# A fused transformer kernel's last up projection: VectorE's sums of weights ahead of its other work, taps counted by chunk, and the last tile's channels read at the end

## The chip, the cores and the metric

One core of one Trainium2 chip runs the whole program. The metric is the device time of one execution in microseconds. The engines are TensorE (PE, with its weight loads as PEld), VectorE (DVE), ScalarE (ACT), GpSimd (POOL) and SyncE (SP), which issues most DMAs. Each runs its own list of instructions in order, and semaphores tie the lists together.

## What is computed

Two blocks of a small model follow each other on 256 tokens of width 1024, all in float32: a mixer (mLSTM) and a mixture of experts, a second mixer (GLA) and a second mixture of experts, then attention and a gated feed-forward network with a convolution. The change lies in the last one:

```python
def conv_ffn(y, w_up, conv_w, conv_b, w_down):
    """Gated MLP with causal depthwise conv between up-projection and activation."""
    u = y @ w_up                                   # [256,1024] @ [1024,5632]
    c = u.shape[-1]
    u = lax.conv_general_dilated(u, conv_w[:, None, :], window_strides=(1,),
                                 padding=[(CONV_WIDTH_2 - 1, 0)],
                                 dimension_numbers=('NWC', 'WIO', 'NWC'),
                                 feature_group_count=c) + conv_b
    gate, val = jnp.split(u, 2, axis=-1)
    return (jax.nn.silu(gate) * val) @ w_down      # [256,2816] @ [2816,1024]
```

CONV_WIDTH_2 is 3. The result is added to the stream, and a last RMS norm follows.

## The kernel before

**Tiles of the up projection.** The 2816 gate channels and the 2816 value channels are cut into UPT = 11 tiles of 256 of each. A tile has four chunks c of 128 channels: 0 and 1 are gates, 2 and 3 values. Tile 0 is projected alone (L1330) into banks 0 and 1. The other ten go in five pairs, `UPS`, called blocks 0 to 4 here (g in the code), each one use of a seven-product scheme: the matrices are halved along tokens, along the inner dimension and along columns, and seven products of sums and differences of the parts stand in for eight plain ones.

**TensorE.** `block_product(u, x)` (L891) issues product x in four steps k of four matmuls; the trace has two records for each matmul. The order is 1, 2, 3, 6, 5, 7, 4. Products 1 to 3 read weights as they landed. Products 6, 5, 7 and 4 read sums of weights and wait for them step by step (`weights_summed[2]`, `[1]`, `[3]`, `[4]`). Product 6 adds to the bank of product 1 and waits for the first take; product 7 adds to the same bank and waits for the fourth (`out_taken`, 9u+4). Odd and even blocks use different banks.

**Who makes the sums.** GpSimd makes the four first sums (L685) and the eight last ones (L694) of each block, one after another. VectorE makes the four second ones in `second_weight_sums` (L1728), each in place in the weights that product 3 reads, so that sum k waits for step k of product 3. GpSimd's last sums read VectorE's.

**VectorE.** `take_value(u, number, x, tt, j)` (L1768 for a copy, L1770 for an addition) brings product x out of its bank into `pre[0]` or `pre[1]`, nine takes in all for a block: takes 1 and 2 are of products 1 and 2, take 3 of 3, take 4 of 6, takes 5 and 6 of 5, takes 7 and 8 of 7 (`middle_values` is takes 4 to 8), take 9 of 4 (`last_values`). Take 1 overwrites `pre[0]`, so it waits for the convolution of the tile before that lay there. After take 7 the odd tile s = 2g+1 is whole in `pre[1]`, after take 9 the even tile s = 2g+2 in `pre[0]`.

**The convolution.** For tile s of `CONV_ORDER` = 0, 2, 1, 4, 3, 6, 5, 8, 7, 10, 9, ACT makes the middle tap and the bias of the four chunks (L1626), VectorE adds the two other taps in two passes of four steps (`convolve`, L2181), ACT takes silu of the gates (L1630), and VectorE multiplies gates and values (`gated`, L2190) into `ffh`, with one count of `ff_ready` for each tile. `conv` has two buffers, so the taps of tile s wait for `ff_ready` of s-2.

**The down projection.** `product` (L1359) is again seven products, of 11 matmuls of 512 columns each. Matmul p of product 1 reads the first of tile p's two channel blocks, and `down_step` counts six weight tiles of two matmuls each (the last has one). Product 1 waits for `ff_ready` once a weight tile, for `min(2 * i + 3, UPT)`. Product 3 waits for sums of the left operand that VectorE makes once all tiles are gated (L2213 to L2218); then VectorE makes the sums of the right operand (L2221, L2263, L2269, L2274), adds products to the stream (L2238), and the norm ends the program.

Of the kernel before, what the change touches and what calls it, by code (L numbers as in the profile page):

```python
# [18 lines left out]
ACT = mybir.ActivationFunctionType  # L19
# [121 lines left out]
def build_in(nc, t, out, ctx):  # L141
# [660 lines left out]
    def _(pe):  # L802
# [515 lines left out]
        def ffn():  # L1318
            turn_only(acc, U_FFN, 0)
            arrived(pe, T_UP)  # L1320
            w = slot(T_UP).rearrange("p (k n) -> p k n", k=KC)
            for tt in range(TT):
                for c in range(4):
                    at = (c % 2) * S + tt * P
                    if (tt, c) == (0, 3):
                        turn_only(acc, U_FFN, 1)
                    for k in range(KC):
                        if c == 0 and k % 4 == 0:
                            turned_bank(U_FFN, 2 * tt + k // 4)
                        last = mm(PS[c // 2][:, at:at + P], w[:, k, c * P:(c + 1) * P], xT[:, k, tt * P:(tt + 1) * P],  # L1330
                                  start=(k == 0), stop=(k == KC - 1), skip_group_check=True)
            last.then_inc(tile_used, 1)
            pe.wait_ge(small_landed[4], 64)
            for j in range(4):
                last = turn(PS[6][:, j * 2 * FB:(j + 1) * 2 * FB], conv_rows[:, j, :], ident[0:2 * FB, 0:2 * FB])
            last.then_inc(convT_done, 1)
            for u in UPS:
                for x in (1, 2, 3, 6, 5, 7, 4):
                    if (u, x) == (UPS[0], 3):
                        pe.wait_ge(convT_copied, 1)  # L1340
                    elif (u, x) == (UPS[1], 1):
                        pe.wait_ge(conv_done, 1)
                    block_product(u, x)

            def product(x, left, odd, half, bank, first=True):

                made = {3: 4, 4: 2, 5: 1, 6: 2, 7: 3}
                for i in range(N_DOWN):
                    if x == 1:
                        pe.wait_ge(ff_ready, min(2 * i + 3, UPT))  # L1350
                        arrived(pe, T_DOWN + i)
                    elif x == 4:
                        pe.wait_ge(right_ready[4], i + 1)
                    elif x in (5, 6, 7):
                        pe.wait_ge(right_ready[made[x]], i + 1)
                    w = right_block(i, odd, half)
                    for r in range(w.shape[1]):
                        p = 2 * i + r
                        last = mm(PS[bank][:, :], left[:, p], w[:, r], start=(first and p == 0), stop=(p == PAIRS - 1),  # L1359
                                  skip_group_check=True)  # L1360
                    last.then_inc(down_step, 1)

            pe.wait_ge(out_taken, 9 * UPS[-1] + 6)
            product(1, left_block(0, 0), 0, 0, 6)
            product(2, left_block(0, 1), 1, 0, 7)
            pe.wait_ge(left_ready, 3)
            pe.wait_ge(out_taken, 9 * (UPS[-1] + 1))
            product(3, left_sum(4), 1, 1, 4)

            pe.wait_ge(sums_taken, 1)  # L1370
            product(6, left_sum(2), 1, 1, 6, first=False)
            product(5, left_sum(1), 0, 1, 5)
            pe.wait_ge(left_ready, 4)
            pe.wait_ge(sums_taken, 4)
            product(7, left_sum(3), 0, 0, 6, first=False)
            product(4, left_block(1, 1), 1, 0, 7)
# [14 lines left out]
    def _(act):  # L1391
# [215 lines left out]
        def ffn():  # L1607
            for tt in range(TT):
                rms_root(1, tt)
                copy_turned(U_FFN, tt)  # L1610
            act.wait_ge(convT_done, 1)
            f(convw_t, PS[6][:, 0:8 * FB], ACT.Copy).then_inc(convT_copied, 1)
            act.wait_ge(convT_copied, 1)

            for s, i in enumerate(CONV_ORDER):
                if s == 0:
                    act.wait_ge(tile_used, T_UP + 1)
                else:

                    act.wait_ge(out_taken, 9 * UPS[(s - 1) // 2] + (7 if s % 2 else 9))  # L1620
                if s >= 2:
                    act.wait_ge(ff_ready, s - 1)
                for c in range(4):
                    n = 2 * i + c % 2 + FB * (c // 2)
                    src = PS[c // 2][:, (c % 2) * S:(c % 2 + 1) * S] if s == 0 else pre[s % 2][:, c]
                    last = f(conv[:, s % 2, c], src, ACT.Identity, scale=conv_cols[:, 2, n:n + 1],  # L1626
                             bias=conv_cols[:, 3, n:n + 1])
                last.then_inc(taps_done, 1)
                act.wait_ge(conv_done, s + 1)
                f(conv[:, s % 2, 0:2], conv[:, s % 2, 0:2], ACT.Silu).then_inc(ff_silu, 1)  # L1630

            f(small[:, 250:251], ones[:, 0:1], ACT.Sqrt, bias=rms_eps)
            for i, (tt, j) in enumerate(((0, 0), (0, 1), (1, 1), (1, 0))):
                c = slice(512 * j, 512 * (j + 1))
                act.wait_ge(final_sum, i + 1)
                f(acc[:, tt, c], x_tok[:, tt, c], ACT.Square, accum_out=half_squares[:, 2 * tt + j:2 * tt + j + 1]
                  ).then_inc(final_square, 1)
                if i == 1:
                    final_deviation(0)
            final_deviation(1)  # L1640
# [18 lines left out]
    def _(dve):  # L1659
# [509 lines left out]
        def ffn():  # L2169
            copy_transposes(U_FFN)  # L2170
            dve.wait_ge(convT_copied, 1)

            def convolve(s):
                i = CONV_ORDER[s]
                dve.wait_ge(taps_done, s + 1)
                for back in (1, 2):
                    for c in range(4):
                        n = 2 * i + c % 2 + FB * (c // 2)
                        u = PS[c // 2][:, (c % 2) * S:(c % 2 + 1) * S - back] if s == 0 else pre[s % 2][:, c, 0:S - back]
                        dst = conv[:, s % 2, c, back:S]  # L2180
                        last = v.scalar_tensor_tensor(dst, u, conv_cols[:, 2 - back, n:n + 1], dst, ALU.mult, ALU.add)  # L2181
                    if back == 1:
                        link(last)
                last.then_inc(conv_done, 1)

            def gated(s):
# [10 lines left out]
            for g, u in enumerate(UPS):  # L2197
                dve.wait_ge(conv_done, 2 * g + 1)
                take_value(u, 1, 1, 0, 0, None)
                gated(2 * g)  # L2200
                take_value(u, 2, 2, 0, 0)
                second_weight_sums(u)
                take_value(u, 3, 3, 0, 1, None)
                middle_values(u)
                convolve(2 * g + 1)
                last_values(u)
                gated(2 * g + 1)
                convolve(2 * g + 2)
            gated(UPT - 1)

            dve.wait_ge(ff_ready, UPT)
            dve.wait_ge(tile_used, T_UP + UPT)
# [115 lines left out]
```

## Time and profile before

| | |
|---|---|
| median of 3 runs | 1548.99 us (1548.19 to 1549.23) |
| the profiled execution | 1550.7 us, its span 1548.7 us |
| mean granted TensorE clock | 0.933 |
| busy share of the span | PE 82%, PEld 47%, DVE 33%, ACT 14%, POOL 20% |
| chain that ended last | PE 49%, DMA 38%, DVE 7% |
| up projection in five blocks, the first at | 1335.56 us |
| down projection, first matmul at | 1472.68 us |

Shares are of the whole program, whose long middle is the two mixtures of experts; what a change in the feed-forward network is worth has to be read between 1335 us and the end. All durations come from the one profiled execution. A row of the timeline may merge several instructions (xN), and its own duration then runs from the start of the first to the end of the last. Matmuls overlap each other, so a product's length is read from start to start.

### The profile page before, as it was taken

The page shows a single profiled execution, that of the slowest core. Times are in us where ns is not written, and L with a number is a line of the kernel's source. Part 1 is how long each engine was busy: PE and PEld are TensorE (multiplying, and loading weights), DVE is VectorE, ACT ScalarE, POOL GpSimd, SP SyncE. Part 2 cuts the span into 40 slices and gives each one's busy share as a digit, 9 for nine tenths or more (in the row PEclk, how much of TensorE's full clock was granted, in tenths as well). Part 3 has the DMA queues.
Part 4 walks back from the last instruction along what each step waited for, and adds up shares of the span by engine and source line. Part 5 has one row for each costly group of instructions (what it writes and reads, how often), then busy time and mean ns, then how long its engine had stood idle before and what let it go on. Part 6 is the DMA issues. An engine that isn't in the chain of part 4 may idle for free.

```text
span 1548.7 us, 21551 instructions
## 1 busy us (share of the span) xinstructions
PE 1273.6 (82%) x9321; PEld 733.3 (47%) x9321; DVE 505.3 (33%) x980; ACT 214.9 (14%) x440; POOL 313.9 (20%) x274
## 2 busy tenths in 40 slices
PE   9998977567667679999887667767768999998998
PEld 7554533223223234865533223223224784998943
DVE  2457210001001006677311000001005456567684
ACT  1032100000000001261200000000002014121110
POOL 2404000000000006574000000000001757355600
PEclk9999999889788899999998988888889999999999
DMA  9928899999999999736799999999999980444000
GB/s 347 384 96 320 331 427 427 429 427 427 428 426 427 427 419 369 304 116 231 312 427 427 428 426 427 427 427 427 427 427 388 313 264 30 160 141 186 28 0 28
DMA packets 88286, 498.89 MB, mean 322 GB/s; under 512 B 8452, under 2 KB 31392, under 8 KB 63872
## 3 DMA queue, kind: packets, MB, share of 16 engines
q1 hardware_dynamic: 85728, 490.23, 78.1%
q0 software_dynamic: 2464, 7.29, 1.5%
q8 instruction: 74, 1.21, 0.3%
q14 instruction: 20, 0.16, 0.0%
HBM read 496.42 MB, written 1.07 MB: 321 GB/s over the span
## 4 chain that ended last, share of the span: by engine, by line
PE 49%; DMA 38%; DVE 7%; another core or an unknown queue 2%; issue 1%; ACT 1%; SPq 0%; DVEq 0%; POOL 0%
DMA weight_ring<-in_moe_w_down 29%; PE bank L891 12%; PE bank L894 7%; PE bank L1182 5%; PE bank L1359 4%; PE bank L1247 4%; PE bank L1234 4%; PE bank L857 3%; DMA weight_ring<-in_moe_w_up 3%; DMA phase_room<-in_moe_w_gate 3%; DMA weight_ring<-in_moe_w_gate 3%; DVE weight_ring L1728 2%; PE bank L1157 1%; PE bank L1330 1%
## 5 line engine op out<-in xcount | busy, mean ns | idle before, releaser
L1182 PE MATMUL bank<-weight_ring,x_tok 128*32 128x256 f32 x3328 | 225.7, 420 | 111.9 <-DMA weight_ring<-in_moe_w_up 95.2
L1182 PEld LDWEIGHTS bank<-weight_ring,x_tok 128*32 128x32 f32 x3328 | 110.8, 118 | 222.4 <-issue 87.0
L1234 PE MATMUL bank<-weight_ring,xT 128*32 128x512 f32 x864 | 136.9, 765 | 75.2 <-DMA weight_ring<-in_moe_w_down 69.1
L694 POOL TENSOR_TENSOR weight_ring<-weight_ring 128x512 f32<-128x512 f32 x112 | 152.6, 1394 | 153.2 <-DVE weight_ring L1728 87.1
L685 POOL TENSOR_TENSOR weight_ring<-weight_ring 128x512 f32<-128x512 f32 x56 | 73.0, 1335 | 455.6 <-DMA weight_ring<-in_w_qkv 442.2
L2073 DVE TENSOR_TENSOR xT<-xT,bank 128x256 f32<-128x256 f32 x32 | 13.5, 421 | 460.7 <-PE bank L1182 460.7
L1247 PE MATMUL bank<-x_tok,xT 128*128 128x512 f32 x256 | 124.5, 630 | 0.0
L2078 DVE COPY x_tok<-bank 128x512 f32<-128x512 f32 x32 | 22.1, 692 | 249.9 <-PE bank L1234 249.9
L1234 PEld LDWEIGHTS bank<-weight_ring,xT 128*32 128x32 f32 x864 | 27.1, 124 | 155.4 <-DMA weight_ring<-in_moe_w_down 71.9
L1247 PEld LDWEIGHTS bank<-x_tok,xT 128*128 128x128 f32 x256 | 49.1, 203 | 87.2 <-issue 87.2
L720 POOL DMA_DIRECT2D phase_room<-in_gla_w_in x1 | 1.0, 967 | 434.2 <-PE bank L1234 434.2
L891 PE MATMUL bank<-xT,weight_ring 128*128 128x128 f32 x768 | 87.7, 275 | 0.0
L891 PEld LDWEIGHTS bank<-xT,weight_ring 128*128 128x128 f32 x768 | 86.8, 192 | 1.0 <-issue 1.0
L891 PE MATMUL bank<-acc,weight_ring 128*128 128x128 f32 x640 | 75.3, 277 | 8.9 <-DVE weight_ring L1728 8.9
L891 PEld LDWEIGHTS bank<-acc,weight_ring 128*128 128x128 f32 x640 | 72.8, 192 | 11.1 <-DVE phase_room L1770 6.8
L1182 PE MATMUL bank<-phase_room,x_tok 128*32 128x256 f32 x768 | 51.2, 416 | 23.7 <-DMA phase_room<-in_moe_w_up 17.1
L894 PE MATMUL bank<-weight_ring,xT 128*128 128x512 f32 x144 | 66.7, 609 | 2.2 <-issue 1.4
L1728 DVE TENSOR_TENSOR weight_ring<-weight_ring 128x512 f32<-128x512 f32 x56 | 65.5, 1219 | 2.4 <-PE bank L891 1.6
L857 PE MATMUL bank<-weight_ring,xT 128*128 128x512 f32 x128 | 59.0, 594 | 0.6 <-PE bank L857 0.6
L894 PE MATMUL bank<-weight_ring,acc 128*128 128x512 f32 x128 | 57.1, 597 | 1.1 <-DVE weight_ring L1728 1.1
L1554 ACT ACTIVATE xT<-bank 128x256 f32<-128x256 f32 x32 | 12.3, 384 | 272.3 <-PE bank L1209 272.3
L1182 PEld LDWEIGHTS bank<-phase_room,x_tok 128*32 128x32 f32 x768 | 25.8, 117 | 48.9 <-issue 17.7
(299 smaller groups left out, 1514.7 us busy)
## 6 DMA issues: line engine op xcount, KB each, us to landing
weight_ring<-in_moe_w_gate SPq DMA_DIRECT2D x52, 2048.0 KB, 49.7
weight_ring<-in_moe_w_up SPq DMA_DIRECT2D x52, 2048.0 KB, 49.7
weight_ring<-in_moe_w_down SPq DMA_DIRECT2D x52, 2048.0 KB, 49.3
phase_room<-in_moe_w_gate SPq DMA_DIRECT2D x12, 2048.0 KB, 48.1
phase_room<-in_moe_w_up SPq DMA_DIRECT2D x12, 2048.0 KB, 50.0
weight_ring<-in_w_up SPq DMA_DIRECT2D x22, 1024.0 KB, 10.5
phase_room<-in_moe_w_down SPq DMA_DIRECT2D x8, 2048.0 KB, 50.4
weight_ring<-in_gla_w_in SPq DMA_DIRECT2D x6, 2048.0 KB, 23.4
```

Of the source, the lines that this page charges most:

```text
L685: nc.gpsimd.tensor_tensor(a, a, b, ALU.subtract).then_inc(weights_summed[1], 1)
L694: nc.gpsimd.tensor_tensor(b, a, b, ALU.subtract).then_inc(weights_summed[x], 1)
L857: last = mm(bank[:, :], xT[:, k, tt * P:(tt + 1) * P], w[:, k, :], start=(k == 0), stop=(k == KC - 1), skip_group_check=True)
L891: last = mm(bank[:, c * P:(c + 1) * P], w[:, k, c * P:(c + 1) * P], left[:, k], start=(first and c == 0), stop=(k == HALF - 1), skip_group ...
L894: last = mm(bank[:, :], left[:, k], w[:, k], start=first, stop=(k == HALF - 1), skip_group_check=True)
L1157: last = mm(PS[quarter % 2][:, at:at + P], x_perm[:, tt, k, :], sels[g][:, tt], start=(tt == 0), stop=(tt == TT - 1))
L1182: last = mm(bank[q * CAP:(q + 1) * CAP, 0:S], xinT[:, 4 * r + k, j * CAP:(j + 1) * CAP], w[k][:, q * S:(q + 1) * S], start=(r == 0 and k = ...
L1234: last = mm(PS[i][k * CAP:(k + 1) * CAP, :], hidT[:, 4 * r + k, :], w[k][:, i * 512:(i + 1) * 512], start=(r == 0), stop=(r == 1), skip_gr ...
L1247: last = mm(PS[4 + 2 * tt + i][:, :], selT[:, tt * P:(tt + 1) * P], exp_t[:, i * 512:(i + 1) * 512], start=False, stop=True, skip_group_ch ...
L1359: last = mm(PS[bank][:, :], left[:, p], w[:, r], start=(first and p == 0), stop=(p == PAIRS - 1), skip_group_check=True)
L1728: v.tensor_tensor(a, a, b, ALU.subtract).then_inc(weights_summed[2], 1)
L2078: v.tensor_copy(exp_t[:, 512:1024], PS[1][:, :]).then_inc(exp_dve, 1)
```

## The change

Three edits of order. In the loop over blocks VectorE does the second sums of weights straight after take 1, then take 2, and then the gated products, of which the odd tile's has moved into the next block (and behind everything for the last tile). ACT counts every tap chunk, VectorE waits chunk by chunk (for tile 0 for all four), and take 9 stands between the two passes of the odd tile's convolution; ACT makes silu of an odd tile only behind the taps of the even one after it. In product 1 of the down projection each matmul waits for its own tile only, and pair 9, whose tile is convolved last, is read last.

```diff
             def product(x, left, odd, half, bank, first=True):
                 made = {3: 4, 4: 2, 5: 1, 6: 2, 7: 3}
-                for i in range(N_DOWN):
+                blocks = [(i, r) for i in range(N_DOWN) for r in range(right_block(i, odd, half).shape[1])]
+                if x == 1:
+                    blocks.append(blocks.pop(UPT - 2))
+                for i, r in blocks:
+                    p, w = 2 * i + r, right_block(i, odd, half)
                     if x == 1:
-                        pe.wait_ge(ff_ready, min(2 * i + 3, UPT))
+                        pe.wait_ge(ff_ready, CONV_ORDER.index(p) + 1)
                         arrived(pe, T_DOWN + i)
-                    elif x == 4:
+                    elif x == 4 and r == 0:
                         pe.wait_ge(right_ready[4], i + 1)
-                    elif x in (5, 6, 7):
+                    elif x in (5, 6, 7) and r == 0:
                         pe.wait_ge(right_ready[made[x]], i + 1)
-                    w = right_block(i, odd, half)
-                    for r in range(w.shape[1]):
-                        p = 2 * i + r
-                        last = mm(PS[bank][:, :], left[:, p], w[:, r], start=(first and p == 0), stop=(p == PAIRS - 1),
-                                  skip_group_check=True)
-                    last.then_inc(down_step, 1)
+                    last = mm(PS[bank][:, :], left[:, p], w[:, r], start=(first and (i, r) == blocks[0]),
+                              stop=((i, r) == blocks[-1]), skip_group_check=True)
+                    if r == w.shape[1] - 1:
+                        last.then_inc(down_step, 1)
...
# ScalarE
-                    last = f(conv[:, s % 2, c], src, ACT.Identity, scale=conv_cols[:, 2, n:n + 1],
-                             bias=conv_cols[:, 3, n:n + 1])
-                last.then_inc(taps_done, 1)
-                act.wait_ge(conv_done, s + 1)
-                f(conv[:, s % 2, 0:2], conv[:, s % 2, 0:2], ACT.Silu).then_inc(ff_silu, 1)
+                    f(conv[:, s % 2, c], src, ACT.Identity, scale=conv_cols[:, 2, n:n + 1],
+                      bias=conv_cols[:, 3, n:n + 1]).then_inc(taps_done, 1)
+                if s % 2 == 0:
+                    for done in range(max(s - 1, 0), s + 1):
+                        act.wait_ge(conv_done, done + 1)
+                        f(conv[:, done % 2, 0:2], conv[:, done % 2, 0:2], ACT.Silu).then_inc(ff_silu, 1)
...
# VectorE
-            def convolve(s):
+            def convolve(s, between=None):
                 i = CONV_ORDER[s]
-                dve.wait_ge(taps_done, s + 1)
                 for back in (1, 2):
                     for c in range(4):
+                        dve.wait_ge(taps_done, 4 * s + c + 1 if s else 4)
...
                     if back == 1:
                         link(last)
+                        if between is not None:
+                            last_values(between)
                 last.then_inc(conv_done, 1)
...
                 take_value(u, 1, 1, 0, 0, None)
-                gated(2 * g)
+                second_weight_sums(u)
                 take_value(u, 2, 2, 0, 0)
-                second_weight_sums(u)
+                for s in range(max(2 * g - 1, 0), 2 * g + 1):
+                    gated(s)
                 take_value(u, 3, 3, 0, 1, None)
                 middle_values(u)
-                convolve(2 * g + 1)
-                last_values(u)
-                gated(2 * g + 1)
+                convolve(2 * g + 1, between=u)
                 convolve(2 * g + 2)
-            gated(UPT - 1)
+            for s in (UPT - 2, UPT - 1):
+                gated(s)
```

## Rows read from the trace of the kernel before

**Rows 1.** Chain that ended last, from 1335 us: start us, us, what.
```profile
1335.63 35.94 PE bank L891 x320
...
1371.68 0.68 DVE phase_room L1770
...
1483.05 59.51 PE bank L1359 x138
```

**Rows 2.** Windows: stretch, us, busy us of each engine, PEclk, DMA share, GB/s.
```profile
1335.56:1360.60 25.04, 25.04 (x226) 25.04 (x225) 17.06 (x26) 6.24 (x11) 15.10 (x12) 1.00 0.27 85
...
1371.60:1399.60 28.00, 25.78 (x224) 25.24 (x224) 19.27 (x32) 5.38 (x10) 16.00 (x12) 1.00 0.41 156
...
1472.68:1483.05 10.37, 7.03 (x18) 2.85 (x16) 8.12 (x19) 4.06 (x7) 0.00 (x0) 1.00 0.00 0
```

**Rows 3.** Waits of TensorE, 1335 to 1549 us: total us, times, longest.
```profile
PE bank L891 <- DVE weight_ring L1728: 8.9, 12, 1.5
PE bank L1359 <- DVE phase_room L2190: 3.3, 1, 3.3
```

**Rows 4.** Timeline, block 0, T = 1342.81: start us, us, engine, line, operation, count.
```profile
1342.81 14.46 PE L891 MATMUL bank<-acc,weight_ring 128*128 128x128 f32 x128
1343.97 0.69 DVE L1728 TENSOR_TENSOR weight_ring<-weight_ring 128x512 f32<-128x512 f32 x1
1344.81 1.27 POOL L694 TENSOR_TENSOR weight_ring<-weight_ring 128x512 f32<-128x512 f32 x1 [24.48 <-PE bank L891]
1344.87 1.76 DVE L1728 TENSOR_TENSOR weight_ring<-weight_ring 128x512 f32<-128x512 f32 x1 [0.20 <-PE bank L891]
1344.87 4.04 DVE L1728 TENSOR_TENSOR weight_ring<-weight_ring 128x512 f32<-128x512 f32 x3 [0.20 <-PE bank L891]
1346.77 9.40 POOL L694 TENSOR_TENSOR weight_ring<-weight_ring 128x512 f32<-128x512 f32 x7 [0.69 <-DVE weight_ring L1728]
1347.15 1.75 DVE L1728 TENSOR_TENSOR weight_ring<-weight_ring 128x512 f32<-128x512 f32 x1
1350.16 0.69 DVE L1770 TENSOR_TENSOR norm_rows<-norm_rows,bank 128x512 f32<-128x512 f32 x1 [0.65 <-PE bank L891]
1356.14 4.97 POOL L685 TENSOR_TENSOR weight_ring<-weight_ring 128x512 f32<-128x512 f32 x4
```

**Rows 5.** Timeline, block 1, T = 1367.82.
```profile
1370.41 0.69 DVE L1768 COPY phase_room<-bank 128x512 f32<-128x512 f32 x1
1372.28 4.63 DVE L1728 TENSOR_TENSOR weight_ring<-weight_ring 128x512 f32<-128x512 f32 x4
1376.96 8.30 PE L891 MATMUL bank<-acc,weight_ring 128*128 128x128 f32 x72 [0.51 <-DVE weight_ring L1728]
```

**Rows 6.** Timeline, from the end of block 0's product 7 on.
```profile
1357.10 10.88 PE L891 MATMUL bank<-xT,weight_ring 128*128 128x128 f32 x96
1357.31 0.69 DVE L1770 TENSOR_TENSOR norm_rows<-norm_rows,bank 128x512 f32<-128x512 f32 x1 [2.09 <-PE bank L891]
1358.03 2.08 ACT L1626 ACTIVATE phase_room<-norm_rows,phase_room 128x256 f32<-128x256 f32 x4 [15.35 <-DVE norm_rows L1770]
1358.10 0.69 DVE L1768 COPY phase_room<-bank 128x512 f32<-128x512 f32 x1
1360.14 1.25 DVE L2181 SCALAR_TENSOR_TENSOR phase_room<-norm_rows,phase_room 128x255 f32<-128x255 f32 x1 [1.35 <-ACT phase_room L1626]
```

**Rows 7.** Timeline, last block's end and the down projection, X = 1472.68.
```profile
1478.24 3.37 DVE L2181 SCALAR_TENSOR_TENSOR phase_room<-phase_room 128x255 f32<-128x255 f32 x8 [1.35 <-ACT phase_room L1626]
1481.64 0.63 ACT L1630 ACTIVATE phase_room<-phase_room 128x512 f32<-128x512 f32 x1 [3.44 <-DVE phase_room L2181]
...
1486.35 1.62 DVE L2217 TENSOR_TENSOR weight_ring<-phase_room,weight_ring 128x1408 f32<-128x1408 f32 x1
...
1489.43 6.36 DVE L2221 TENSOR_TENSOR weight_ring<-weight_ring 128x1024 f32<-128x1024 f32 x6
```

**Rows 8.** Timeline of SyncE's DMA issues: start us, us until the last landed.
```profile
1361.91 83.32 SPq L553 DMA_DIRECT2D weight_ring<-in_w_down  x6
```

## The prediction

> **What bounds the kernel now.** I read the chain that ended last first, because it says which engine the end waits for in the part that the change touches, from about 1335 us on [rows 1]. It is TensorE's row of matmuls, broken in five places by VectorE: four times by a take and the sums of weights (L1770, L1728), once, at 1469, by the road of the last tile (take, taps, convolution, silu, product) into the down projection. No DMA stands in it. The windows say the same: TensorE is at full granted clock in every stretch, the block from 1335.56 takes 25.04 us, and the block from 1371.60, with the same work (224 records against 226), 28.00 us [rows 2]. The next two have 28.00 as well (two more rows of the same pattern). So each later block loses 3.0 us. The list of waits has only two entries for TensorE here, on L1728 and on L2190 [rows 3].
>
> Why one block is whole and the others are not is seen in the timeline. Let T be the first record of product 3 of a block and X the end of its product 4, where the next block starts. In the whole block (T = 1342.81) products 3, 6, 5, 7 run without a gap up to 1357.10, so a product takes 14.29/4 = 3.57 us and one of its four steps k 0.89 [rows 4]. VectorE's first sum starts at T+1.16 and the last ends at T+6.10 [rows 4]; product 6 wants the last at T+3.57+2.68 = T+6.25, so it comes just in time. In the next block (T = 1367.82) VectorE comes out of the convolution of tile 2g, does take 1, waits for its silu, does the gated product and take 2, and only then, at T+4.46, the first sum; product 6 should start at T+3.57 and its last step starts at 1376.96, T+9.14, 2.89 late [rows 5].
>
> **The change part by part.** All is edited order; no arithmetic, DMA or matmul is added or taken away.
>
> *Sums ahead.* In blocks 1 to 4 the first sum now follows take 1. What can hold it: product 3's first step (T+0.89, and a wake-up), or VectorE's row before it. Block 0 shows the first case: T+1.16. For the second I go back from T. Take 7 starts 0.21 after product 7 ends (1357.10 to 1357.31), its four ACT taps 0.72 after that (2.08 for the four, so one each 0.5), take 8 at 1358.10 [rows 6]. Now the first pass of the odd tile's convolution follows tap by tap instead of after the last tap. But GpSimd is then at its four first sums (L685, until 1361.11 in block 0) [rows 4, 6], and the rows show how the two engines meet. A sum of VectorE that starts 0.06 us behind a GpSimd operation (1344.81, 1.27 long) takes 1.76 us instead of 0.69, ending 0.55 after it [rows 4]; a convolution step that starts at 1360.14, in GpSimd's last L685, takes 1.25 instead of some 0.42 (3.37 for eight without GpSimd [rows 7]) and ends 0.28 after it [rows 4, 6]. Takes, with one operand in PSUM, keep 0.69 beside GpSimd [rows 4]. So they alternate, one operation each. With that the first pass ends at about X+2.0: three steps each behind one GpSimd operation (4.97/4 = 1.24). Then take 9 (0.7) to X+2.7, the second pass 1.7 to X+4.4, the even tile's eight steps 3.4 [rows 7] to X+7.8, take 1 to X+8.4. The first sum may start there, as X+8.4 is T+1.2 (X to T is two products, 7.15). That is where block 0 has it, to 0.1 or 0.2 us. **The 2.99 us of four blocks go: 11.96 us**, less about 0.1 each for this tie.
>
> *Gated products behind take 2.* From block 1 on, two of them (both operands in SBUF) now stand between take 2 and take 3, while GpSimd is in its eight last sums (9.40 us from T+3.96 on) [rows 4]. Product 7 accumulates on the bank that take 4 reads, so TensorE waits for take 4; it wants it at T+3x3.57 = T+10.72. VectorE: sums to T+6.1, take 2 to 6.7, the first gated product behind GpSimd's operation that ends at T+7.22, to T+7.8; GpSimd to 9.0; the second to 9.6; take 3 from 9.55, take 4 from 10.34 (two takes in a row that wait on each other start 0.79 apart, 1357.31 and 1358.10 [rows 6]), to 11.0; 0.15 to wake TensorE. That is T+11.15, **0.3 to 0.4 late: a new wait of product 7**, in each of blocks 1 to 4. In the trace of before take 4 ends at 1350.85, T+8.04 [rows 4], 2.7 us ahead of product 7: that was the cover of everything between take 2 and take 4, and the two gated products and take 2 eat it up. Behind the waiting product nothing else is held: take 5 and on shift with it. With the 0.1 above, 0.43 a block, **1.7 us in all**. It is bounded below by 0 (neither tie costs) and above by about 1.6 a block: VectorE 0.5 later out of the convolution and one more GpSimd operation ahead of each gated product. I take 0.43, the value of the row-by-row walk.
>
> The Trainium skill weighs on exactly this ("SBUF — State Buffer", Who interferes with whom): a VectorE operation with two inputs in SBUF and a GpSimd operation that reads SBUF exclude one another for their whole length, the second waiting till the first is done. Read as a shared bandwidth instead, the mean of a sum beside GpSimd (4.04/3 = 1.35 us) would be all that a gated product costs, take 4 would come about 0.2 sooner, and the total would be some 1 us less. The single operations (1.76, then a short one, then 1.75) agree with the lock.
>
> *Other edits of order.* Silu of the odd tile moves behind the even tile's taps, which frees ACT for these taps at take 9 and not after silu (0.63 us [rows 7]). A tap counts singly: four increments for one, and VectorE waits before each step; a step's start-to-start is 0.42, waits included, and I cost a wait that is already met at nothing. At the most it is the 0.10 by which the 0.79 of the two takes is over their 0.69: 1.6 a block for 16 steps, which VectorE would hand on to the first sum; the upper bound above covers it once. ACT's wait for ff_ready before new taps (L1622) now meets gated products of the block before, done by T+9.6, while taps start at T+15. Slots of weights fall free earlier, but the last issue of the down weights landed by 1445.23 [rows 8], and product 1 will read them from about 1462 on: nothing.
>
> *The tail.* X = 1472.68 for the last block. GpSimd is idle there [rows 2]. Now: 8 matmuls of product 1 (one is 59.51/69 = 0.86, two records each [rows 1]), 6.9 us, then a stand until 1483.05, X+10.37: **3.5 us idle by start times** (3.3 by the wait's own row [rows 3]). After: the first pass of tile s = 9 ends at X-0.1 (last tap at X-0.57), take 9 from X+0.2 to 0.9, the taps of s = 10 from X+0.93, one each 0.5, VectorE's second pass to X+2.55, tile 10's eight steps to X+5.92, silu 0.63, the two gated products: the first at X+5.9 to 6.6, the second to X+7.3, TensorE told at X+7.36 (lengths from [rows 7]). Product 1 now has nine matmuls that need neither, to X+7.73, then pair 10 (ready X+6.6), then pair 9 (wanted at X+8.59, ready X+7.36). **The stand goes whole: 3.5 us.** What is late next: the left sums. They are done at 1486.35+1.62 = 1487.97, 4.9 after the last gated product, which let TensorE go at 1483.05 [rows 1, 7]; after, at X+12.2; product 3 wants them at X+22x0.86 = X+18.9. The differences of L2221 end at X+20.2 (before at 1495.79, X+23.1 [rows 7]), 1.3 instead of 0.6 after product 3's start; six sums of the same shape for product 6 follow, 6.4 us in all (the 6.36 of L2221), behind two additions; product 6 starts at X+28.3 and asks for the first, done by X+23.2. Nothing stops TensorE.
>
> **Sum.** 11.96 + 3.5 - 1.7 = 13.8, and 0.1 for one refill of TensorE that I can't place: 13.7 us. The profiled execution: span 1548.7, 1550.7 with what lies around it, 1.7 above the median 1548.99. Taking the difference off, the span would be 1535.0, and the **median 1535.3** (0.9% less). No cost: 1548.99-15.5 = 1533.5. Upper bound of the new waits: 1548.99-15.4+6.4 = 1540.0.
>
> **Rivals.**
> *VectorE becomes the row that sets the block.* If the convolution's first pass meets GpSimd on all four steps and the second pass too, the first sum comes 1 to 2 us late, and each microsecond beyond T+1.3 goes to product 6 and again to T of the next block. For: VectorE has no slack by my walk. Against: GpSimd's first sums are at an end by X+1.5. At 1.5 a block with the 0.4: 15.4-7.6 = 7.8, 1541 us.
> *GpSimd keeps its row.* If VectorE's gated product had to let GpSimd's eight last sums through, not one, it would start at T+13.4 and take 4 end at about T+16: 5.3 us a block, 21 in all against 15.4 gained, so **1554.9, slower**. It decides from 3.9 us a block on. Against: at 1347.15 VectorE waits for one operation only, with six to come [rows 4].
> *The sums don't come sooner* because something other than their place holds them (the convolution of 2g, as take 1 starts only at 1370.41, T+2.59, in block 1 [rows 5]). In the trace take 1 was late because take 9, silu and taps ran in series behind eight contended steps. If that stays, sums start at T+3.3 and two thirds stay lost: 15.4-8 = 7.4, 1541.6; if all of it stays, the tail's 3.5 less 1.5 of new waits is all: 1547, no difference that could be told.
> *The clock.* It is 1.00 in the block without a pause as in those with one [rows 2]; more blocks of the first kind give it no reason to fall. I give it no chance of its own.
>
> **Chances.** The walk, with new waits of 0 to 1.6 a block: 0.84, its own range 1533.4 to 1540.0. VectorE's row sets the block, or the sums don't come so much sooner (1540 to 1546): 0.09. Within 0.2% (3.1 us, about what a measurement of this kernel can tell from no change): 0.04. Slower: 0.03. So faster 0.93, same 0.04, slower 0.03; range 1533.0 to 1540.5, which leaves out about 0.15 above and a little below.
>
> **What would show it.** Right: blocks 1 to 4 at 25.4 us from product 3 to product 3, VectorE's first L1728 at T+1.2, no wait of product 6 but one of 0.3 to 0.4 us of product 7 on take 4 (L1770), a single unbroken piece of L1359 from X on, and take 9 before the second four steps of the convolution. Wrong: a wait on L1728 of a microsecond or more, GpSimd operations three in a row while VectorE stands at L2190, a gap in product 1 or 3, or the granted clock below 1.00 after 1335 us.

## The result, and the profile after

| | before | after |
|---|---|---|
| median, first comparison (4 and 4 runs) | 1549.11 us | 1536.1 us (1534.07 to 1537.55) |
| ratio, 95% interval | | 0.9911 (0.9892 to 0.9931) |
| median, second comparison (9 and 5 runs) | 1550.71 us | 1534.26 us (1532.38 to 1537.56) |
| ratio, 95% interval | | 0.9900 (0.9886 to 0.9913) |
| profiled execution | 1550.7 us, span 1548.7 | 1534.07 us, span 1532.1 |
| product 1 of block 0 to the last take of the stream (L2238, now L2246) | 207.02 us | 192.65 us |

The prediction was 1535.3 us in 1533.0 to 1540.5, and both medians lie in that range. The last row of the table is the measure that the rest uses. It runs from the first record of the first block to the last addition to the stream (1335.56 to 1542.58 before, 1333.31 to 1525.96 after) and I call it the stretch. It holds all that the change can move: 14.37 us less. The spans differ by 16.6; 2.25 of that lies ahead of the stretch, where nothing was changed. One execution of the kernel before, timed beside four of the experiments, took 4275.83 us, far from all others, and is left out of their ratios.

The chain that ended last, after (start us, us, what), answers to [rows 1]. VectorE is gone from it until the last addition: the whole of the five blocks and of the down projection is TensorE's.

```profile
1333.38 43.08 PE bank L891 x384
1376.46 0.07 issue
1376.52 25.25 PE bank L891 x224
...
1401.83 25.25 PE bank L891 x224
...
1452.44 7.38 PE bank L891 x64
1459.83 66.11 PE bank L1361 x154
```

The windows of the same stretches (us, busy us of PE, PEld, DVE, ACT, POOL, clock, DMA share, GB/s) answer to [rows 2]. The first is block 0, the second block 1 from product 3 to product 3, the third the tail.

```profile
1333.31:1358.42 25.11, 25.11 (x226) 25.11 (x225) 18.93 (x27) 6.24 (x11) 15.17 (x12) 1.00 0.26 85
1365.58:1390.89 25.31, 25.25 (x227) 25.08 (x225) 22.14 (x31) 5.31 (x10) 16.85 (x12) 1.00 0.46 173
...
1459.66:1525.90 66.24, 66.24 (x156) 29.14 (x154) 45.75 (x55) 7.27 (x15) 0.00 (x0) 1.00 0.02 8
```

A later block takes 25.31 us instead of 28.00. The list of TensorE's waits, which had 8.9 and 3.3 us [rows 3], has one entry of 0.3 us from 1300 us on, ahead of the stretch. The 0.30 us by which a later block is longer than block 0 (25.02 from product 3 to product 3) stands in neither list; it is read from start to start, and in part from a weight load below. VectorE is busy for 22.1 us of a block's 25.3, what GpSimd adds to its operations included: it is close to being the bound itself.

The timeline of block 2, T = 1390.89, and the end of block 1, X = 1383.74, shows how it runs now (start us, us, engine, line, operation, count); it answers to [rows 4 to 6].

```profile
1379.80 5.32 POOL L685 TENSOR_TENSOR weight_ring<-weight_ring 128x512 f32<-128x512 f32 x4
1381.77 4.02 DVE L2187 SCALAR_TENSOR_TENSOR phase_room<-norm_rows,phase_room 128x255 f32<-128x255 f32 x4
1385.83 0.69 DVE L1775 TENSOR_TENSOR phase_room<-phase_room,bank 128x512 f32<-128x512 f32 x1
1388.01 3.36 DVE L2187 SCALAR_TENSOR_TENSOR phase_room<-phase_room 128x255 f32<-128x255 f32 x8
1390.89 14.75 PE L891 MATMUL bank<-acc,weight_ring 128*128 128x128 f32 x128
1391.41 0.69 DVE L1773 COPY phase_room<-bank 128x512 f32<-128x512 f32 x1
1392.05 0.69 DVE L1733 TENSOR_TENSOR weight_ring<-weight_ring 128x512 f32<-128x512 f32 x1
1392.95 4.03 DVE L1733 TENSOR_TENSOR weight_ring<-weight_ring 128x512 f32<-128x512 f32 x3 [0.20 <-PE bank L891]
1397.50 1.16 DVE L2198 TENSOR_TENSOR phase_room<-phase_room 128x512 f32<-128x512 f32 x1
1398.07 1.72 POOL L694 TENSOR_TENSOR weight_ring<-weight_ring 128x512 f32<-128x512 f32 x1
1398.58 1.75 DVE L2198 TENSOR_TENSOR phase_room<-phase_room 128x512 f32<-128x512 f32 x1
1401.04 0.69 DVE L1775 TENSOR_TENSOR norm_rows<-norm_rows,bank 128x512 f32<-128x512 f32 x1
1401.80 3.65 PEld L891 LDWEIGHTS bank<-acc,weight_ring 128*128 128x128 f32 x32 [0.22 <-issue]
```

Read it from the top. The first pass of the odd tile's convolution (four steps in 4.02 us, between GpSimd's first sums) ends at X+2.05, take 9 follows at once, the even tile's eight steps end at X+7.63, take 1 is at T+0.52 and the first sum at T+1.16. The two gated products take 1.16 and 1.75 us where one alone takes 0.69, and take 4 ends at T+10.84. The weight loads of product 7 start right behind it, at T+10.91, after a stand of 0.22 us.

### The profile page after: what moved, and what is told of

It reads as the page before. It is cut to its first block, busy times and chain, and to the rows that moved or that the text cites. A ratio compares the mean times of both kernels' runs of the same rounds, so it can differ in the third digit from the quotient of the medians.

```text
span 1532.1 us, 21562 instructions
## 1 busy us (share of the span) xinstructions
PE 1273.3 (83%) x9321; PEld 732.9 (48%) x9321; DVE 518.0 (34%) x980; ACT 214.3 (14%) x440; POOL 318.2 (21%) x274
## 4 chain that ended last, share of the span: by engine, by line
PE 52%; DMA 38%; DVE 6%; another core or an unknown queue 2%; issue 1%; ACT 1%; SPq 0%; DVEq 0%; POOL 0%
DMA weight_ring<-in_moe_w_down 24%; PE bank L891 13%; PE bank L894 7%; DMA weight_ring<-in_moe_w_up 6%; PE bank L1182 6%; PE bank L1361 4%; PE bank L1247 4%; PE bank L1234 4%; PE bank L857 3%; DMA phase_room<-in_moe_w_down 3%; DMA weight_ring<-in_moe_w_gate 3%; PE bank L1157 1%; PE bank L1330 1%; PE bank L1101 1%
## 5 line engine op out<-in xcount | busy, mean ns | idle before, releaser
L1234 PE MATMUL bank<-weight_ring,xT 128*32 128x512 f32 x864 | 142.1, 791 | 76.2 <-DMA weight_ring<-in_moe_w_down 70.0
L694 POOL TENSOR_TENSOR weight_ring<-weight_ring 128x512 f32<-128x512 f32 x112 | 154.9, 1413 | 134.6 <-PE bank L891 79.0
L685 POOL TENSOR_TENSOR weight_ring<-weight_ring 128x512 f32<-128x512 f32 x56 | 75.2, 1373 | 458.8 <-DMA weight_ring<-in_w_qkv 443.1
L2083 DVE COPY x_tok<-bank 128x512 f32<-128x512 f32 x32 | 22.1, 692 | 256.9 <-PE bank L1234 256.9
L1562 ACT ACTIVATE x_tok<-bank 128x512 f32<-128x512 f32 x32 | 19.1, 597 | 205.1 <-PE bank L1234 205.1
```

Of the source, the lines that this page charges most:

```text
L685: nc.gpsimd.tensor_tensor(a, a, b, ALU.subtract).then_inc(weights_summed[1], 1)
L694: nc.gpsimd.tensor_tensor(b, a, b, ALU.subtract).then_inc(weights_summed[x], 1)
L1234: last = mm(PS[i][k * CAP:(k + 1) * CAP, :], hidT[:, 4 * r + k, :], w[k][:, i * 512:(i + 1) * 512], start=(r == 0), stop=(r == 1), skip_gr ...
L1562: f(exp_t[:, 0:512], PS[0][:, :], ACT.Copy).then_inc(exp_act, 1)
L2083: v.tensor_copy(exp_t[:, 512:1024], PS[1][:, :]).then_inc(exp_dve, 1)
```

## The experiments

Each is read by its stretch, by T to T in blocks 1 to 4, and where several executions were timed by the ratio of its median to that of the kernel before. All in one table first (T to T and stretch in us):

| kernel | T to T | stretch | ratio (95%) |
|---|---|---|---|
| before | 28.00 | 207.02 | |
| after, two traces | 25.31 | 192.65, 192.65 | 0.9911, 0.9900 |
| gated products behind take 4 | 25.01 | 191.47 | 0.9894 (0.9879 to 0.9909) |
| tiny last sums (part left out) | 25.01 | 191.46 | |
| old read order | 25.31 | 193.13 | 0.9909 (0.9894 to 0.9925) |
| sums last | 26.30 | 196.60 | 0.9929 (0.9912 to 0.9945) |
| take 9 last | 25.89, 26.03, 26.05 | 195.43 | 0.9919 (0.9904 to 0.9934) |
| taps by tile | 25.73, 25.86, 25.87 | 195.13 | 0.9927 (0.9910 to 0.9943) |
| a third product | 26.98 | 199.35 | |
| before, with the new read order | 28.00 | 205.29 | 0.9986 (0.9977 to 0.9996) |
| before, with the sums moved, two traces | 26.99, 27.02 | 205.94, 203.13 | 0.9986, 0.9982 |
| the same, its stand filled | 27.02 | 203.14 | 0.9974 (0.9963 to 0.9985) |

**The changed kernel again.**

> The changed kernel once more, beside the others of this call. Theory (the walk of the prediction): the stretch from product 1 of block 0 to the last matmul is 192.6 us as in its first trace (1333.31 to 1525.93), with a stand of 0.30 us in each of blocks 1 to 4; the part before it, which the change does not touch, differs from trace to trace by a microsecond or two and is what moves the medians between runs. Rival: the gain itself differs from run to run. Then the stretch would.

The stretch was 192.65 us again, to the hundredth (1336.76 to 1529.41), though it began 3.45 us later in the program. So the stretch of the changed kernel repeats, and what differs between its two traces is the part ahead of it. The kernel before has one trace only, but the kernel with the new read order alone, which has its five blocks, took the same 129.87 us from T of block 0 to X of block 4. Over the fourteen traces of this case the first record of block 0 comes between 1331.94 and 1336.76 us, with the same instructions up to there.

**Where the last 0.30 us of a block is.**

```diff
                 second_weight_sums(u)
                 take_value(u, 2, 2, 0, 0)
-                for s in range(max(2 * g - 1, 0), 2 * g + 1):
-                    gated(s)
                 take_value(u, 3, 3, 0, 1, None)
-                middle_values(u)
+                take_value(u, 4, 6, 0, 1)
+                for s in range(max(2 * g - 1, 0), 2 * g + 1):
+                    gated(s)
+                ...  # takes 5 to 8
```

> In blocks 0 to 4 the gated products stand behind take 4 and not ahead of take 3; all else as in the changed kernel. Theory: the 0.30 us that each later block is longer than block 0 is product 7 waiting for take 4, which the two gated products, each behind one GpSimd operation, push to T+10.84. Then the wait goes, T to T falls from 25.31 to 25.01 us, and the whole gains 1.2 us on the changed kernel; take 5 starts no later than T+11.1. Rival: the 0.30 us is on the sums (product 6). Then the blocks stay at 25.3.

It did that: T to T 25.01, stretch 191.47, 1.18 less. TensorE's rows and VectorE's in block 2 (T = 1389.22):

```profile
1389.22 14.46 PE L891 MATMUL bank<-acc,weight_ring 128*128 128x128 f32 x128
...
1396.81 0.69 DVE L1775 TENSOR_TENSOR norm_rows<-norm_rows,bank 128x512 f32<-128x512 f32 x1
1397.41 2.50 DVE L2198 TENSOR_TENSOR phase_room<-phase_room 128x512 f32<-128x512 f32 x2
1400.14 0.69 DVE L1775 TENSOR_TENSOR norm_rows<-norm_rows,bank 128x512 f32<-128x512 f32 x1 [0.23 <-PE bank L891]
```

Products 3, 6, 5, 7 take 14.46 us again and not 14.75. Take 4 ends at T+8.28, the gated products run in what was VectorE's idle time, and take 5 waits for product 5 and not for them. Of the kernels that compute the whole it has the shortest stretch. By the medians (1533.79 against 1534.26 us, on the same chip) the difference of 1.2 us can't be told.

**Is it GpSimd that stretches the gated products?**

```diff
+                    if u in UPS:
+                        a, b = a[:, 0:1], b[:, 0:1]
                     nc.gpsimd.tensor_tensor(b, a, b, ALU.subtract).then_inc(weights_summed[x], 1)
```

> GpSimd's eight last sums of weights in O_ATT's successors, the five blocks of the up projection, work on one column of 512, so that products 7 and 4 of the up projection use wrong weights: that part is left out. Theory (VectorE and GpSimd exclude one another): with GpSimd's eight operations gone the sums 2 to 4 are held only by the steps of product 3, take 4 waits for product 6 (T+7.4), and T to T is 25.01 us. GpSimd's four first sums move to T+4.6 and meet the gated products, which may still take 1.2 to 1.7 us each. Rival (the 0.30 us is VectorE's own row, whatever GpSimd does): 25.3 stays.

The two gated products, in the same place as in the changed kernel, took 1.29 us together instead of 2.83, each sum its 0.69, and product 7's wait was gone. That GpSimd's first sums would meet the gated products was wrong: they came just behind them.

```profile
1392.90 14.46 PE L893 MATMUL bank<-acc,weight_ring 128*128 128x128 f32 x128
...
1397.58 1.71 POOL L696 TENSOR_TENSOR weight_ring<-weight_ring 128x1 f32<-128x1 f32 x5 [0.70 <-DVE weight_ring L1735]
1397.96 1.29 DVE L2200 TENSOR_TENSOR phase_room<-phase_room 128x512 f32<-128x512 f32 x2
1399.25 4.95 POOL L685 TENSOR_TENSOR weight_ring<-weight_ring 128x512 f32<-128x512 f32 x4
```

**One more product in that place.**

```diff
+                if twice:  # s is the odd tile's, blocks 1 to 4; unused_room stands for a stretch of room
+                    v.tensor_tensor(unused_room, conv[:, s % 2, 0:2], conv[:, s % 2, 2:4], ALU.mult)
                 v.tensor_tensor(ffh[:, 2 * i:2 * i + 2, :], conv[:, s % 2, 0:2], conv[:, s % 2, 2:4], ALU.mult
                                 ).then_inc(ff_ready, 1)
```

> The changed kernel with one more product of VectorE (both operands in SBUF, 128x512, written to unused room) ahead of the first gated product in blocks 1 to 4. Theory (VectorE and GpSimd alternate, one operation each): it costs one GpSimd operation and its own length, 1.67 us, all of it on take 4: product 7 waits 1.97 instead of 0.30, T to T 26.9 to 27.0 us. Rival (they share a bandwidth, or VectorE takes its turn freely): 0.6 to 1.35 us more, T to T 25.9 to 26.65. Rival (GpSimd keeps its row): over 5 us.

T to T was 26.98 (1379.34 to 1406.32, product 7 to product 7), 1.67 more. VectorE's rows are the extra product (L2199) and the two real ones (L2200); TensorE stood 1.73 us before product 7, which the profile lists under "issue".

```profile
1400.31 1.16 DVE L2199 TENSOR_TENSOR phase_room<-phase_room 128x512 f32<-128x512 f32 x1
1401.40 3.43 DVE L2200 TENSOR_TENSOR phase_room<-phase_room 128x512 f32<-128x512 f32 x2
...
1406.32 3.81 PE L891 MATMUL bank<-acc,weight_ring 128*128 128x128 f32 x32 [1.73 <-issue]
```

So an operation of 0.69 us costs 1.67 there, one turn of both engines. That is less than the two lengths alone, 0.69 and 1.27, which add to 1.96: the records show VectorE's operation ending 0.54 us behind GpSimd's (1400.33 and 1399.79 in the trace of after), not 0.69. Neither a mean price of 1.35 nor a row of GpSimd that is let through first fits.

**The read order: in the changed kernel, and alone.**

```diff
-                    blocks.append(blocks.pop(UPT - 2))
...
-                        pe.wait_ge(ff_ready, CONV_ORDER.index(p) + 1)
+                        pe.wait_ge(ff_ready, min(2 * i + 3, UPT))
...  # and the two loops over i and r as before
```

> Product 1 of the down projection as before: waits by weight tile and pair 9 in its place; the rest as changed. Theory: TensorE comes to the fifth weight tile at X+6.9 and is let go by the last gated product at X+7.25, so it stands 0.4 us and the whole is 0.4 us longer than the changed kernel: the new read order is worth little once VectorE's road is short. Rival: the read order carries the tail's gain of 3.6 us; then 3 us or more come back.

> The kernel before with the new product 1 of the down projection (a wait for each tile, pair 9 last) and nothing else. Theory: the last gated product is still at X+9.6, so TensorE stands until X+10.37 as before, but with ten of its eleven matmuls done instead of eight: the stand falls from 3.5 to 1.8 us, and the whole gains 1.7 us; the four waits for sums stay (T to T 28.00 us). Rival: the order is what makes the tail's gain; then 3.5 us.

Taken out of the changed kernel it cost 0.48 us (193.13 against 192.65); put into the kernel before it gave 1.73. TensorE's rows of product 1, first of the former, then of the latter:

```profile
1459.19 7.03 PE L1359 MATMUL bank<-weight_ring,phase_room 128*128 128x512 f32 x16
1466.43 12.28 PE L1359 MATMUL bank<-weight_ring,phase_room 128*128 128x512 f32 x28 [0.21 <-DVE phase_room L2195]
```

```profile
1472.86 8.75 PE L1361 MATMUL bank<-weight_ring,phase_room 128*128 128x512 f32 x20
1483.23 10.57 PE L1361 MATMUL bank<-weight_ring,phase_room 128*128 128x512 f32 x24 [1.62 <-DVE phase_room L2193]
```

In the one there are eight matmuls before a stand of 0.2 us, in the other ten before one of 1.6. The worth of the order depends on how late VectorE is, and once its road was short most of it was gone. By the medians the latter is 0.14% faster than the kernel before (interval 0.04 to 0.23%).

**The place of the sums: alone, and taken back.**

```diff
                 take_value(u, 1, 1, 0, 0, None)
-                gated(2 * g)
-                take_value(u, 2, 2, 0, 0)
                 second_weight_sums(u)
+                take_value(u, 2, 2, 0, 0)
+                gated(2 * g)
```

> The kernel before with the order take 1, sums of weights, take 2, gated product in each block and nothing else. Theory: take 1 stays at T+2.6, where the series take 9, silu, taps, eight steps leaves it, so the first sum comes at T+3.2 instead of T+4.46, and the last at T+7.9; product 6 still waits some 1.8 us. T to T falls from 28.00 to 26.7 or 26.8 us, 5 us in all, and the tail stays: under half of what the changed kernel gains. Rival: the place of the sums is the whole cause; then 25.0 to 25.3 and 11 us.

```diff
-                second_weight_sums(u)
                 take_value(u, 2, 2, 0, 0)
                 for s in range(max(2 * g - 1, 0), 2 * g + 1):
                     gated(s)
+                second_weight_sums(u)
```

> The changed kernel with take 2 and the two gated products ahead of the sums again. Theory: take 1 ends at T+1.2, take 2 and two gated products (0.64 each, GpSimd idle) put the first sum at T+3.1 and the last at T+7.8: product 6 waits 1.5 to 1.8 us, T to T 26.6 us, 5 us more than the changed kernel. With the run of the sums alone: each half leaves 1.5 to 1.8 us a block standing, and only both together clear it. Rival: the shorter convolution road alone clears the sums; then 25.0 to 25.3.

Alone the move took a block to 26.99, 1.0 off and not the 1.2 to 1.3 I had put down. Taken back it cost 0.99 a block and not 1.3, since the first sum came at T+2.74 and not T+3.1. Both agree that moving the sums is worth about 4 us of the 14.4, in either direction, and the other edits in the changed kernel give 10.4 without it. VectorE's rows show what each leaves over, first the sums alone (T = 1369.00), then sums last (T = 1390.63):

```profile
1371.84 0.69 DVE L1768 COPY phase_room<-bank 128x512 f32<-128x512 f32 x1
1372.44 4.63 DVE L1728 TENSOR_TENSOR weight_ring<-weight_ring 128x512 f32<-128x512 f32 x4
```

```profile
1390.77 0.69 DVE L1773 COPY phase_room<-bank 128x512 f32<-128x512 f32 x1
1391.56 0.69 DVE L1775 TENSOR_TENSOR phase_room<-phase_room,bank 128x512 f32<-128x512 f32 x1
1392.16 1.29 DVE L2198 TENSOR_TENSOR phase_room<-phase_room 128x512 f32<-128x512 f32 x2
1393.37 4.63 DVE L1733 TENSOR_TENSOR weight_ring<-weight_ring 128x512 f32<-128x512 f32 x4
```

In the first, take 1 itself is late (T+2.84), so the sums can't be early. In the second, take 1 is at T+0.14, and 1.9 us of other work stands between it and them.

**What shortened the road to take 1.**

```diff
-                convolve(2 * g + 1, between=u)
+                convolve(2 * g + 1)
+                last_values(u)
```

> The changed kernel with take 9 behind both passes of the odd tile's convolution instead of between them. Theory: take 9 starts at X+3.7 instead of X+2.1, ACT's taps of the even tile behind it, so that VectorE now waits for taps; take 1 comes at X+8.7, the first sum at T+2.2, and product 6 waits 0.8 to 0.9 us in blocks 1 to 4: T to T 26.1 us, 3.4 us in all. The tail stays whole (last gated product done at X+7.9, wanted at X+8.6). Rival: VectorE has slack there; then 25.3 stays.

```diff
-                        dve.wait_ge(taps_done, 4 * s + c + 1 if s else 4)
+                        dve.wait_ge(taps_done, 4 * s + 4)
```

> The changed kernel, but VectorE waits for all four taps of a tile before its first step. Theory: the first pass then starts at X-0.55 instead of X-1.97, but GpSimd's first sums held it up anyway, so it ends at X+2.3 instead of X+2.05; the even tile's steps start when its four taps are done, X+5.2, instead of X+4.6. The first sum is then 0.5 to 0.9 us late and T to T 25.5 to 26.0 us: 1 to 3 us in all; the tail stays whole. Rival: chunk counts are a large part of the shorter road; then 26.5 or more.

Take 9 last: 25.89 to 26.05 a block (forecast 26.1), and 2.8 us in all instead of 3.4. Taps by tile: 25.73 to 25.87 a block (forecast 25.5 to 26.0) and 2.5 us in all, of which 0.4 in the tail, where I had said none. VectorE's rows there (X = 1461.74) show it: the even tile's steps wait 0.57 us for the fourth tap, and the last gated product ends at 1470.48, X+8.74, where pair 9 is wanted at X+8.6.

```profile
1463.50 1.66 DVE L2187 SCALAR_TENSOR_TENSOR phase_room<-norm_rows,phase_room 128x254 f32<-128x254 f32 x4
1465.73 3.37 DVE L2187 SCALAR_TENSOR_TENSOR phase_room<-phase_room 128x255 f32<-128x255 f32 x8 [0.57 <-ACT phase_room L1629]
1469.01 1.47 DVE L2198 TENSOR_TENSOR phase_room<-phase_room 128x512 f32<-128x512 f32 x2
```

The edits other than the place of the sums gave 1.70 us a block (28.00 to 26.30), more than either of these two. The other two parts of VectorE's road, silu of the odd tile behind the even tile's taps and the odd tile's gated product in the next block, were not taken back one by one: what each is worth, and how the 3.6 us of the tail divide beyond the 0.5 of the read order, stays open.

**The clock behind the stand.** The first trace of the kernel before with the sums moved gained 4.0 us in the blocks and lost 2.96 of it in the tail. Its windows show why. The first holds eight matmuls of product 1 and then TensorE's stand (1476.85 to 1480.20); the others lie behind it:

```profile
1469.80:1480.20 10.40, 7.05 (x19) 2.88 (x17) 8.15 (x19) 4.07 (x7) 0.00 (x0) 0.96 0.00 0
1480.20:1484.00 3.80, 3.80 (x5) 1.73 (x6) 3.73 (x3) 0.81 (x2) 0.00 (x0) 0.50 0.00 0
1484.00:1488.00 4.00, 4.00 (x8) 1.56 (x8) 4.00 (x4) 0.00 (x0) 0.00 (x0) 0.73 0.00 0
1488.00:1492.00 4.00, 4.00 (x11) 1.85 (x10) 4.00 (x4) 0.00 (x0) 0.00 (x0) 1.00 0.00 0
```

The granted clock is at its lower level, 1.2 GHz (0.50 of 2.4), when TensorE starts again, and the 14 matmuls there take 15.1 us instead of 12.1. In narrower windows it is 1.00 until 1479.2, 0.88 in the next 0.2 us and 0.50 from 1479.4 on: it fell inside the stand, some 2.5 us behind the last matmul's record. It is 1.00 again from 1486.2 on. So TensorE worked at half the clock for 6.0 us, which costs 3.0 us: what the tail lost. Two more runs bear on that: the same kernel once more, and the same with its stand filled.

```diff
                     if x == 1:
+                        if i == 4:
+                            keep_busy(7, PS[0])
                         pe.wait_ge(ff_ready, min(2 * i + 3, UPT))
```

> The kernel before with only the sums moved, once more. In its first trace the granted clock fell to 0.50 and 0.73 for 8 us right after the stand ahead of the last gated product, and 14 matmuls took 15.1 us instead of 12.1. Theory: the stand of 3.35 us brings the fall, in some executions at the least; the stretch is then 205.9 us with it or 203.0 without. Rival: the fall has nothing to do with the stand; then it comes anywhere or not at all.

> The same kernel with seven matmuls of 128x256 on constants, into a bank that nobody reads, ahead of TensorE's wait in product 1 (they fill 3.0 of the 3.5 us of the stand). Theory: with the stand filled the clock stays 1.00 there, the 14 matmuls behind it take 12.1 us, and the stretch is 203.0 us; the median is 1 to 3 us below the kernel without them if the fall is usual there. Rival: the filling changes nothing, or costs what the matmuls overrun.

The second trace had a stand of 3.38 us and no fall (stretch 203.13), nor had the trace of the kernel before, with one of 3.34; with the stand filled there was none either (203.14). The medians are 1547.67 us for 12 runs (1542.9 to 1550.08) and 1546.24 for 7 filled ones (1545.41 to 1547.28). The intervals of their ratios to the kernel before overlap, but these runs were timed together, and eleven of the twelve are slower than six of the seven filled ones. That would fit falls that are common without the filling, but the part ahead of the stretch moves these times too, and two traces without it, one with a fall and one without, don't show how common they are. That the fall comes in one execution and not in another of the same kernel is shown.

## Why the prediction held, step by step

- **The five blocks.** 2.99 us of stand in each of blocks 1 to 4 were to go, less 0.43 of new waits, to 25.4 a block. Measured 25.31, so 0.30 is left and 10.77 us were gained from T of block 0 to X of block 4 (129.87 to 119.10), against 10.2.
- **VectorE's road.** First pass done at X+2.0 (measured X+2.05), even tile done at X+7.8 (X+7.63), first sum at T+1.2 (T+1.16). The 0.1 a block put down for this tie was not there. That three of its links matter, the experiments on them show: 0.99 a block for the place of the sums, 0.6 to 0.7 for take 9, 0.4 to 0.6 for the taps. The links of silu and of the odd tile's gated product have no run of their own.
- **Product 7's new wait.** 0.3 to 0.4 us behind the two gated products. Measured 0.30, with the first ending at T+7.77 (walk: 7.8), the second at T+9.44 (9.6), take 4 at T+10.84 (11.0). Three experiments place it: it goes when the products stand elsewhere, it goes when GpSimd's operations are tiny, and it grows by one turn of both engines when one more product stands there. The prediction's sign for it, a wait on take 4 in the profile's list, didn't come: the list has no such row, and the 0.30 is seen from start to start.
- **The tail.** 3.5 us. Measured 3.60 (69.90 to 66.30 from X to the last addition to the stream). The last gated product ended at 1466.85, X+7.19 against X+7.3. The rest of the tail hid as forecast: no wait of product 3 or 6.
- **The sum.** 13.7 forecast, 14.37 in the stretch; the 0.67 too few are, but for rounding, 0.13 a block of waits, 0.1 of the tail and the 0.1 that I had called a refill, for which no row shows anything. The median fell by 13.0 us in one comparison and 16.45 in the other, while the changed kernel's stretch was the same to 0.01 us. So for its part the difference lies ahead of the stretch; for the kernel before, with one trace, the clock below is another candidate. That both medians came within about 1 us of 1535.3 is in part luck, since they differ by 1.8 us between themselves.
- **The rivals.** "VectorE becomes the row that sets the block" didn't come, but it was near: any one of four small delays brings it, at 0.4 to 1.7 us a block more than the 25.31. "GpSimd keeps its row" fell by the trace of after (each gated product behind one operation) and by the third product. "The sums don't come sooner" is what happens in the kernel with the sums alone: 26.99 a block. I had priced that rival at 2.0 of 3.0 lost; it was 1.98.
- **The page of the Trainium skill** ("SBUF — State Buffer", Who interferes with whom) said of two engines with such operands that one waits out the other. The rows of 1.16 and 1.75 us beside GpSimd's 1.72, and 0.65 each without it, agree with that and not with a mean price. For "their whole length", which the prediction took from it, the trace is 0.29 us short: a turn of both took 1.67 us and not 1.96.
- **The clock** was given no chance. In the traces of before and after it was 1.00 in the whole stretch up to the last matmul. But in the first trace with the sums moved it fell inside the stand of the tail, which no other of the fourteen traces shows in the stretch, and I had not thought of the stand that goes as one that can cost more than its length. How often that happens to the kernel before no run shows, and it may be part of why the medians differ by more than the stretch in one comparison. That stays open.

## What to carry to other kernels

When an engine in series with the bound has room in its share but none in its order, walk one period row by row, from the bound's first need back, with each wait's due time: here that gave a new wait of 0.30 us to within 0.1. What an edit of order gives depends on how late the row is with the others in place: the read order gave 1.7 us while VectorE was late and 0.5 once it was nearly on time, whereas the place of the sums gave 4 us with and without the other edits, as VectorE was late in both. Put operations that two engines can't run at once where the waiting one has idle time: behind take 4 the same two products took 2.50 us and cost TensorE nothing.

## What the runs showed of the hardware

- VectorE operations with both operands in SBUF and GpSimd's take turns, one each, when both have a queue of them (128x512, float32): 0.69 us costs 1.67 in the middle of such a row, and GpSimd's 1.27 becomes 1.72. VectorE's with an operand in PSUM keeps 0.69 beside GpSimd's.
- The granted clock of TensorE can fall to 0.50 inside a stand of 3.35 us, some 2.5 us behind the last matmul, stay there for 6.0 us after it and cost 2.96 us, in one execution of a kernel and not in another with a stand of 3.38 us.
- The part of the program ahead of the stretch, bound by DMA for long, ends between 1331.94 and 1336.76 us with the same instructions; the 193 us behind it repeated to 0.01 in the two traces of the changed kernel.
